# Where the softmax sums are divided out: in rows of probabilities instead of in a turned tile of inverse sums

## The reference, cut to what matters

```python
# group A, 8 heads: three dilated windows, merged by their softmax denominators
# group B, 4 heads: indexer scores, causal top-256 keys, attention over those keys
# group M, 4 heads: cross-attention into 256 memory tokens
...
s = jnp.where(valid, s + bias, -jnp.inf)
p = jnp.exp(s - m)
l = jnp.sum(p, axis=-1, keepdims=True)
o = jnp.einsum('brhnqk,brhnkc->brhnqc', p.astype(vb.dtype), vb).astype(jnp.float32) / l
...
o = jnp.concatenate([oA, oB, oM], axis=-1)
o = o * jax.nn.silu(gate)
x = x + o @ w_out[layer]
```

## Time and profile before

| | |
|---|---|
| median of 3 runs | 719.12 us (717.1, 719.12, 721.47) |
| the profiled execution | 717.74 us, span of its instructions 716.0 us |
| TensorE busy | 674.8 us, 94% of the span |
| VectorE busy | 422.4 us, 59% |
| ScalarE busy | 333.2 us, 47% |
| GpSimd busy | 144.4 us, 20% |
| steps 0 to 7 (pair M) | 129.8 to 194.1 us, told by VectorE's `add_bias` |
| steps 8 to 39 (pairs A) | 194.1 to 478.9 us |
| steps 40 to 55 (pairs B) | 478.9 to 594.2 us |
| steps 56 to 63 (pair M), output and last norm | from 594.2 us |

### The profile page before, as it was taken

How to read it: one execution, slowest core, us unless ns; L and a number is a source line. 1 busy time by engine, 2 the same in 40 slices (tenths; PEclk the granted TensorE clock), 3 DMA queues, 4 the chain that set the end, 5 groups by cost and what they waited for, 6 DMA issues and landing times.

```text
span 716.0 us, 11579 instructions
## 1 busy us (share of the span) xinstructions
PE 674.8 (94%) x4281; PEld 538.9 (75%) x4281; DVE 422.4 (59%) x991; ACT 333.2 (47%) x632; POOL 144.4 (20%) x95
## 2 busy tenths in 40 slices
PE   5999999999999999999998999999999999999993
PEld 4788887777778777777776787776888777777772
DVE  4857874396788477976698564553343354122247
ACT  5876653353335442534253434653563585112233
POOL 2021110111323022221124113300111156212101
PEclk9999999999999999999999999999999999999997
DMA  8521120111211131112111121101110416410005
GB/s 279 179 60 30 30 81 9 30 29 45 89 45 46 29 89 45 30 45 89 45 31 44 36 77 47 50 3 45 45 30 24 169 52 225 161 42 22 1 27 209
DMA packets 51863, 47.71 MB, mean 67 GB/s; under 512 B 5712, under 2 KB 44640, under 8 KB 51808
## 3 DMA queue, kind: packets, MB, share of 16 engines
q1 hardware_dynamic: 51808, 46.97, 21.5%
HBM read 39.62 MB, written 7.34 MB: 66 GB/s over the span
## 4 chain that ended last, share of the span: by engine, by line
PE 46%; DVE 13%; issue 3%; ACT 1%; DVEq 0%; ACTq 0%
PE j_ps L1471 13%; PE o_ps L1630 6%; PE pt_ps L1604 5%; PE s_ps L1680 5%; PE s_ps L1471 5%; PE s_ps L1533 4%; PE j_ps L1680 4%; DVE unread L1221 4%; DVE probT L1303 1%; PE s_ps L1686 1%; PE j_ps L1686 1%; DVE prob L1294 1%; DVE tk L1223 1%; PE pt_ps L1652 1%; DVE tk L1222 1%
## 5 line engine op out<-in xcount | busy, mean ns | idle before, releaser
L1471 PE MATMUL j_ps<-h_hi,w_hl 128*128 128x512 f32 (+2 forms) x656 | 213.1, 390 | 4.2 <-DVE h_lo L1080 2.3
L1471 PEld LDWEIGHTS j_ps<-h_hi,w_hl 128*128 128x128 f32 (+1 forms) x656 | 121.2, 186 | 30.0 <-issue 4.4
L713 POOL TENSOR_TENSOR w_hl<-w_raw,w_hl 128x1024 fp32r<-128x1024 f32 (+1 forms) x29 | 69.3, 2388 | 328.3 <-ACT w_hl L815 321.1
L998 ACT ACTIVATE prob<-prob,nmax 128x256 f32<-128x256 f32 (+7 forms) x128 | 90.0, 704 | 83.1 <-DVE nmax L1294 68.8
L1471 PE MATMUL j_ps<-h_lo,w_hl 128*128 128x512 f32 (+2 forms) x328 | 125.4, 382 | 0.0
L986 ACT ACTIVATE probT<-pt_ps 128x512 f32<-128x512 f32 (+3 forms) x88 | 41.2, 469 | 120.3 <-PE pt_ps L1604 119.7
L1604 PE MATMUL pt_ps<-ident,prob 128*128 128x128 f32 x496 | 73.2, 280 | 9.3 <-DVE gate L1321 5.1
L1604 PEld LDWEIGHTS pt_ps<-ident,prob 128*128 128x128 f32 x496 | 54.5, 140 | 26.8 <-issue 19.9
L1471 PE MATMUL s_ps<-h_hi,w_hl 128*128 128x512 f32 x224 | 73.8, 397 | 0.9 <-ACT qk L859 0.9
L1471 PEld LDWEIGHTS j_ps<-h_lo,w_hl 128*128 128x128 f32 (+1 forms) x328 | 61.1, 186 | 11.0
L1221 DVE TENSOR_SCALAR_CACHE_REDUCE unread<-idx,tk 128x384 uint8<-128x384 f32 (+5 forms) x72 | 67.8, 942 | 1.3
(11 more groups left out here) (246 smaller groups left out, 1066.8 us busy)
## 6 DMA issues: line engine op xcount, KB each, us to landing
w_raw<-in_w_in_dram SPq DMA_DIRECT2D x27, 512.0 KB, 3.9
idx<-in_x_dram SPq DMA_DIRECT2D x8, 512.0 KB, 6.3
bias<-in_a_tab_dram SPq DMA_DIRECT2D x8, 512.0 KB, 4.5
mixed_scratch<-gate SPq DMA_DIRECT2D x12, 256.0 KB, 2.4
bias<-in_x_dram SPq DMA_DIRECT2D x4, 512.0 KB, 6.5
probT<-in_w_mem_kv_dram SPq DMA_DIRECT2D x4, 512.0 KB, 6.6
bias<-in_w_out_dram SPq DMA_DIRECT2D x4, 512.0 KB, 4.2
out_dram<-idx SPq DMA_DIRECT2D x4, 512.0 KB, 3.3
```

The lines of the kernel that those rows point to most:

```text
L713: pool.tensor_tensor(w_hl[:, w % 2, 1, :, 0:n], raw_of(w)[:, :, 0:n], w_hl[:, w % 2, 0, :, 0:n].bitcast(F32), ALU.subtract).then_inc(w_lo_ ...
L998: act.activation(prob[:, a, s % 2, 0:n], prob[:, a, s % 2, 0:n], ACT.Exp, scale=-1.0, bias=nmax[:, a, s % 2:s % 2 + 1], accum_out=lsum[:, ...
L1471: last = pe.matmul(bank[0:n, at:], a[:, k, 0:n], c[:, k, HALF * b + at:HALF * b + HALF], start=(k == 0 and q == 0), stop=(k == KD - 1 and ...
```

## The change

The sums are no longer turned. Instead VectorE multiplies each row of probabilities by the inverse of its sum before TensorE transposes it: `even_out(s, a)`, for both heads of each of the 64 steps, placed on VectorE behind `choose_portions(s, 0)` and `copy_probT(s-1, 1)`. It waits for the exponent of its head, takes the reciprocal of one sum, waits for it, and multiplies the row in place with a `tensor_scalar` that also accumulates (its accumulated value, `evened`, is read by nobody). `turn_prob` now waits for `prob_even` instead of `prob_ready`. `invert_sums`, `turn_sums`, the gate's product with the turned sums and the waits on `linv_used` are gone.

```diff
-            groups = [0]
-            def invert_sums(p, g):
-                for a in range(2):
-                    dve.wait_ge(prob_ready[a], p * NT + 4 * g + 4)
-                inverse = lsum[:, p % 2, 4 * g:4 * g + 4, :]
-                link(dve.reciprocal(inverse, inverse))
-                dve.tensor_copy(linv[:, :, :, :], inverse.unsqueeze(3).broadcast_to([P, 4, 2, DH])).then_inc(linv_ready, 1)
-                groups[0] += 1
+            def even_out(s, a):
+                p, i = pair_of_step(s)
+                total = lsum[:, p % 2, i, a:a + 1]
+                row = prob[:, a, s % 2, 0:P * key_tiles(s)]
+                dve.wait_ge(prob_ready[a], s + 1)
+                link(dve.reciprocal(total, total))
+                dve.tensor_scalar(row, row, total, None, ALU.mult, ALU.add, accum_out=evened[:, a:a + 1]).then_inc(prob_even[a], 1)
             def finish_group(p, g):
...
-                dve.wait_ge(linv_turned, groups[0])
                 cut = slice(HALF * g, HALF * g + HALF)
-                dve.tensor_tensor(gates(p)[:, cut], pt_ps[0][:, :, :].rearrange("p a b -> p (a b)"),
-                                  gates(p)[:, cut], ALU.mult).then_inc(linv_used, 1)
-                dve.wait_ge(linv_used, groups[0])
                 dve.wait_ge(pv_done, CHUNK0[p * NT + 4 * g + 4])
                 dve.tensor_tensor(gates(p)[:, cut], o_ps[:, :], gates(p)[:, cut], ALU.mult).then_inc(og_ready, 1)
...
-                if s >= 1 and (s - 1) % 4 == 3:
-                    invert_sums(pair_of_step(s - 1)[0], (s - 1) % NT // 4)
                 choose_portions(s, 0)
                 if early[0]:
                     add_out(*early[0])
                 if s >= 1 and len(chunks(s - 1)) == 2:
                     copy_probT(s - 1, 1)
+                if s < STEPS:
+                    even_out(s, 0)
+                    even_out(s, 1)
...
             def turn_prob(s, c):
...
-                    pe.wait_ge(prob_ready[a], s + 1)
+                    pe.wait_ge(prob_even[a], s + 1)
-                    if a == 0 and s // 4 >= 1:
-                        pe.wait_ge(linv_used, s // 4)
...
-            def turn_sums(s):
-                p, i = pair_of_step(s)
-                pe.wait_ge(linv_ready, s // 4 + 1)
-                pe.wait_ge(pt_ready[0], CHUNK0[s + 1])
-                for c in range(4):
-                    last = pe.transpose(pt_ps[0][:, c, :], linv[:, c, :, :].rearrange("p a f -> p (a f)"), ident[:, :])
-                last.then_inc(linv_turned, 1)
```

More of the change, by code:

```diff
@@ L343, in build_program @@
         lsum = sb("lsum", [P, 2, NT, 2])
-        linv = sb("linv", [P, 4, 2, DH])
+        evened = sb("evened", [P, 2])
         nmax = sb("nmax", [P, 2, 2])
@@ L445, in build_program @@
         pv_done = sem("pv_done")
-        linv_ready = sem("linv_ready")
-        linv_turned = sem("linv_turned")
-        linv_used = sem("linv_used")
+        prob_even = [sem("prob_even_a"), sem("prob_even_b")]
         og_ready = sem("og_ready")
@@ L1638, in turn_values @@
                 pe.wait_ge(pt_ready[0], CHUNK0[s])
-                if s // 4 >= 1:
-                    pe.wait_ge(linv_used, s // 4)
                 n = P if PAIRS[p][0] == "A" else DH
@@ L1733, in _ @@
                     turn_values(s)
-                if s >= 1 and (s - 1) % 4 == 3:
-                    turn_sums(s - 1)
                 if early[2]:
```

## The result

The changed kernel takes 727.94 us (median of 4 runs, 724.99 to 728.53) against 718.98 before: ratio 1.0115, interval 1.0084 to 1.0146, 1.15% slower. The forecast was 727 us, +1.1%. The profiled execution took 724.99 us, span 723.2, against 717.74 and 716.0; it is the fastest of its four, the others lie at 727.5 to 728.5.

The account below looks back on a forecast made before the run. TensorE was taken to set the pace nearly everywhere, VectorE in or near the search's narrow steps. Terms 1.9 + 3.3 + 2.7 + 3.5 - 3.4 = +8.0 us on 717.7, plus 1.4 for the median, gave 727 us; range 717 to 738.

Parts of the forecast that it names:

- a second cost, the place: Multiplications queue behind `choose_portions(s, 0)`, so VectorE may no longer lag TensorE by most of a step; no separate size.
- priced in step 39 alone: Step 39: second head's multiplication ends 0.8 us late, next copy queued behind it about 0.95, counted twice: 1.9 us.
- The four early ones: TensorE's delays: pair M, ending in step 7, +1.9 us; steps 9 to 12 +3.3; 17 to 20 +2.7; 25 to 28 +3.5.
- The last: Steps 32 to 64: group ends and last norm give -6.6 us, search's end and wide steps cost 1.3 and 1.9: -3.4.
- all five stretches: Profile stretches before the change, including steps 9 to 12, 17 to 20, 25 to 28, 34 to 55: clock read as 1.00.
- The first term: Pair M, steps 1 to 7: mostly hidden, but the turn in step 7 waits for its multiplication: +1.9 us.
- The late part: Steps 32 to 64: -6.6 us from group ends and last norm, less 1.3 and 1.9 of costs: -3.4 us.
- the list of signs: Expected in the trace: turns wait 1 to 3 us in steps 7, 10, 11, 17 to 20, 25 to 28; none in 42 to 63.
- Hidden: Rival, whole kernel: VectorE has room, TensorE's 15.2 us all come off, 704 us; chance 0.15.
- Half price: Rival, search steps: accumulating multiplication runs as fast as the plain one, +8.0 becomes about +2, 721 us; chance 0.12.
- Wide steps: Rival, 18 steps i = 5 to 7 of A and B: each loses 0.7 us, 13 us more, 740 us; chance 0.16.

Follow-up runs that it names:

- no division (1): Changed kernel without the row multiplications, TensorE waiting for the exponents and the division left out altogether: 704.16 us, ratio 0.979.
- load without link (2): Changed kernel with the same multiplications written to a row nobody reads, turns waiting for exponents only, output not divided: 721.43 us, ratio 1.0037.
- on ScalarE (4): Changed kernel with the 128 row multiplications moved from VectorE to ScalarE, VectorE keeping the reciprocals: 723.04 us, ratio 1.0066.
- waits filled (8): Changed kernel with 6 to 12 unread identity transpositions before the turns of steps 7, 10, 11, 17, 18, 25 and 27: 723.73 us, ratio 1.0075.
- evenings from 36 (10): Kernel before up to step 35, changed kernel from step 36 on, where the search is over: 716.66 us, ratio 0.9971.
- (7): Changed kernel with a plain multiplication instead of the accumulating one: 730.34 us, ratio 1.0158.
- experiment 6: Changed kernel with the multiplications of steps of up to four key tiles placed ahead of the search's first portions: 723.97 us, ratio 1.0062.
- 3: Kernel before with the same reciprocals and multiplications added on VectorE, written to a tile nobody reads, turned sums kept: 755.27 us, ratio 1.0506.
- 5: Changed kernel with multiplications on ScalarE and the search in (1,2) portions in the second to fourth step of a pair: 720.0 us, ratio 1.0018.
- 9: Changed kernel with one search portion less in each of steps i = 1 to 3 of the A pairs: 719.69 us, ratio 1.0015.
- its control: Kernel before with the search spread thinner, (1,2) portions in steps i = 1 to 3 of the A pairs: 714.49 us, ratio 0.9944.
- 11: Kernel before with the search spread to (1,2) portions and rows multiplied by VectorE from step 40 on: 713.73 us, ratio 0.9924.

## Why the prediction was right, step by step

The table sets every kernel against the one before: by how much the first bias of a step comes later in its trace than in that one's, in us. The last column is the span.

| kernel | step 0 | 9 | 17 | 25 | 33 | 41 | 56 | end |
|---|---|---|---|---|---|---|---|---|
| changed | -0.7 | 1.6 | 3.4 | 5.7 | 9.2 | 9.9 | 9.3 | 7.2 |
| no division (1) | 0.1 | -1.0 | -3.3 | -6.8 | -9.5 | -11.2 | -13.4 | -14.3 |
| load without link (2) | -1.0 | -1.0 | 0.1 | 1.3 | 4.7 | 5.7 | 5.0 | 2.7 |
| on ScalarE (4) | 0.2 | 0.3 | -0.6 | -0.8 | 1.1 | 4.6 | 4.5 | 5.0 |
| waits filled (8) | -1.1 | -0.5 | 1.4 | 3.1 | 6.5 | 7.3 | 6.6 | 4.6 |
| evenings from 36 (10) | 0.0 | 0.1 | 0.1 | 0.1 | 0.4 | 1.7 | 1.0 | -1.0 |

- **The mechanism is shown.** TensorE's share was worth 15 us (1), and the evenings cost more than that where VectorE is full. The loss grows in each pair of the search, by 0.7 us more up to step 41, and not behind that, as forecast. Steps 8 to 39 became 11.3 us longer, not some 9, and from step 40 on 4.1 shorter, not some 3. What the prediction called a second cost, the place, is the smaller one: the link has 6.5 of the 24 us, the load 17 (2), in both of which there is some of the clock. The prediction reckoned each delay from the turn that waits for its evening; with that wait gone most of the delay is still there (5.6 us from mark 9 to mark 33 in the table's row, against 7.6), through waits for VectorE's copies, which it priced in step 39 alone.
- **The terms.** The four early ones were +1.9, +3.3, +2.7, +3.5, together 11.4; the changed kernel's row gives 2.3, 1.8, 2.3 and 3.5 from mark to mark, 9.9. The last was -3.4 and is 7.2 - 9.2 = -2.0. With the 0.7 us by which this trace was early ahead of step 0, where both kernels do the same, the sum is +7.2 for a predicted +8.0. That the total came so near is luck in part: the early terms were 1.5 too high together and the late one 1.4 too low. The stretches themselves grew by 2.8, 2.8 and 4.4 us, and 1.0, 0.7 and 0.9 came back in the wide steps behind them, where the prediction had the delay stay.
- **The clock.** The prediction read 1.00 in all five stretches and priced no change of it. This is the step that failed. The changed kernel ends 2.6 us behind the one with filled waits in the traces (7.2 against 4.6), but 0.4 of that lie ahead of step 0; so the clock costs 2.2 us by the traces, and 4.2 by the medians. Why the medians give more is open: the other three executions of the changed kernel took 2.6 to 3.5 us more than the traced one, but their mean granted clock (0.983 to 0.985, against 0.984) shows no more time at half clock. Of the 2.2, 1.6 fall in pair M, where TensorE sets the pace: 3.4 us at half clock cost about half of that. In the pairs behind they cost 0.5 or less, since VectorE sets the pace and a slower TensorE waits less. The first term is thus +0.6 without the clock, not +1.9: too high a price and a missed one stood against each other.
- **The late part wins back less**, by 1.4 us, and it is the win that was too large. It was put at 6.6 us; without any division (1) it is 14.3 - 9.5 = 4.8. The evenings' cost behind step 33 was put at 1.3 + 1.9 = 3.2 and is 4.8 - 2.0 = 2.8. Step 33 waits 0.89 us and step 39 0.70; step 55 waits 0.69 too, which the sum had (0.95, twice) and the list of signs, with no wait from step 42 on, had not. Experiment 10 bears the size out: 2.1 us in all.
- **Waits.** Steps 7, 10, 11, 17, 18, 25 and 27 wait by 1.1 to 2.1 us, as listed. Steps 19, 20, 26 and 28 were listed too and show 0, 0, 0.50 and 0.34 us. With the waits filled and the clock kept, steps 19, 26 and 28 wait 0.38, 1.78 and 1.18 (8): in the changed kernel the half clock had made TensorE late enough not to wait.
- **VectorE's 503 us, not 513.** The distance of an evening was right (0.74 for 0.76), but gaps were added to busy time: a reciprocal takes 0.158, not the 0.194 of the row with 8 columns, and the 0.04 behind it is idle.
- **Slips.** The 13.0 us idle in pair M are 57.3 less 44.3, and 44.3 is the column of TensorE's weight loads; VectorE has 39.3 there, so 18.0 us idle. The words "mostly hidden" stand, and no term changes. In step 7 the rows give 192.1 - 189.44 = 2.7 us, 3.1 with the 0.4 carried in, where the text has 2.9.
- **Rivals.** Hidden is refuted by the changed kernel itself. Half price falls on 1280 ns, and the plain form that it was taken from would not have given it either, for GpSimd's sake (7). Wide steps show 0.69 and 0.70 in two of 18, and no more.

## What to carry to other kernels

Ask of an added instruction not what its engine is loaded with on average, but who is next in that engine's queue in the narrowest steps: here 17 us of load came out for the larger part as waits for copies that the change never touched, and moving the work to a freer engine gave only 5 back, since that engine has a copy in the chain too. Test load and link apart, in the changed kernel and not in the one before, and look at the clock of every variant before its time is put down to one cause. And make a change only where its engine has room: the same edit costs 9 us over the whole kernel and wins 2 behind the search.

## What the hardware showed

- **Short waits can bring TensorE's clock down.** Behind waits of 2.06, 1.67, 1.81 and 1.76 us the granted clock fell to half for 3.4 us each, with TensorE busy in almost all of it. The wait's length alone doesn't tell: in experiment 6, waits of 2.35, 2.04 and 2.24 us had no such stretch behind them and one of 3.48 had; in the kernel before, waits of 1.60 and 1.76 us had none. Filling the waits kept the clock (8). What decides between these cases stays open. Between executions of one kernel it shows as well: on the chip of experiments 4 and 8, those of the kernel before with a mean granted clock of 0.989 took 719.3 to 720.0 us, those with 0.994 716.9 to 718.1.
- **Stretches of 3.4 us at half clock, step 0 to the last 14 us of each trace:** before 0, changed 4, experiment 1: 0, 2: 3, 3: 7, 4: 2, 5: 5, 6: 2, 7: 6, 8: 0, 9: 1 and in its control 0, 10: 1, 11: 0.
- **The accumulating multiplication** runs at 1280 ns for 1024 columns whatever GpSimd does; the plain one at 808 in the mean, but a row of 128 columns took up to 2.47 us beside GpSimd.
